# A recurrent mixer's gate products in stacked form, with its zero fills and one weight split at other places

## The reference, cut to what matters

```
proj = x @ w_in
gate_b, gate_c, val_a, val_b, gate_lru = split(proj)      # five times 512 channels
y_a = gate_b * causal_conv3(gate_c * val_a)
xc = causal_conv4(val_b) + conv_b_bias
r = sigmoid(xc_heads @ wa + ba)                           # 8 heads of 64 channels
i = sigmoid(xc_heads @ wx + bx)
log_a = -8 * r * softplus(-lam);  a = exp(log_a)
b = sqrt(-expm1(2 * log_a)) * (i * xc)
h[t] = a[t] * h[t-1] + b[t]
y_b = h * gelu(gate_lru)
m = concat(y_a, y_b) @ w_out
x = layer_norm(ALPHA * x + m)
x = layer_norm(ALPHA * x + hier_moe(x))                   # top-1 group, top-2 experts
```

## Time and profile before

| | |
|---|---|
| median of 3 runs | 1199.74 us (1199.53 to 1200.79) |
| the profiled execution | 1202.03 us, of which its span is 1200.3 |
| mean granted clock of TensorE | 0.977 of full speed |
| TensorE busy | 1121.1 us (93% of the span), 5736 matmuls |
| VectorE busy | 808.0 us (67%) |
| ScalarE busy | 537.6 us (45%) |
| GpSimd busy | 194.2 us (16%) |
| first 497 us | the mixer, 20 rounds |

### The profile page before, as it was taken

One profiled execution on the slowest core, in us unless ns is written; L12 is line 12 of the kernel. 1 busy time (PEld: TensorE's weight loads), 2 busy tenths in 40 slices (PEclk: granted clock), 3 DMA queues, 4 the chain that ended last, 5 costly groups with the idle time before them and its releaser, 6 DMA issues.

```text
span 1200.3 us, 20513 instructions
## 1 busy us (share of the span) xinstructions
PE 1121.1 (93%) x5736; PEld 995.4 (83%) x5737; DVE 808.0 (67%) x1532; ACT 537.6 (45%) x703; POOL 194.2 (16%) x189
## 2 busy tenths in 40 slices
PE   6999999999999999999999988899998999999970
PEld 6999999999999999978888867687887887777760
DVE  4666544374446456767777758797755898888884
ACT  4465343363336346422223312655544666656530
POOL 1000000010001000102222223406101132322322
PEclk9999999999999999999999999899999999999995
DMA  5331599747973742544444225896866789888563
GB/s 182 132 107 50 143 147 121 94 114 115 118 91 122 282 170 85 173 140 156 148 168 141 106 93 190 294 330 220 288 232 236 276 320 354 294 297 292 197 225 140
DMA packets 87274, 221.58 MB, mean 185 GB/s; under 512 B 19152, under 2 KB 45808, under 8 KB 80944
## 3 DMA queue, kind: packets, MB, share of 16 engines
q1 hardware_dynamic: 57824, 129.90, 33.1%
q0 software_dynamic: 18160, 59.53, 14.8%
q10 hardware_dynamic: 11232, 31.47, 13.7%
HBM read 133.75 MB, written 87.11 MB: 184 GB/s over the span
## 4 chain that ended last, share of the span: by engine, by line
PE 53%; DMA 16%; DVE 13%; issue 7%; ACT 6%; ACTq 2%; DVEq 2%; SPq 0%; POOL 0%; POOLq 0%
DMA y_scr<-yb 11%; PE ps_h L1484 9%; PE ps_vb_c L903 8%; PE ps_va_b L292 7%; PE ps_vb_c L292 7%; PE ps_va_b L903 6%; PE ps_o L1462 6%; PE ps_g L292 3%; PE ps_x L1451 2%; DMA gate<-g_scr 2%; DVE w_lo L1117 1%; PE ps_r_i L916 1%; ACT x_hi L1112 1%; PE ps_h L1513 1%; DVE yb L562 1%
## 5 line engine op out<-in xcount | busy, mean ns | idle before, releaser
L1484 PE MATMUL ps_h<-x_hi,xt_hi 128*128 x312 | 125.5, 402 | 3.0 <-issue 2.4
L292 PE MATMUL ps_vb_c<-x_hi,w_hi 128*128 (+1 forms) x320 | 114.6, 358 | 9.7 <-DVE x_lo L467 9.6
L1484 PE MATMUL ps_h<-x_hi,xt_lo 128*128 x312 | 122.0, 391 | 0.0
L1484 PE MATMUL ps_h<-w_lo,xt_hi 128*128 x312 | 121.7, 390 | 0.0
L292 PE MATMUL ps_vb_c<-x_hi,w_lo 128*128 (+1 forms) x320 | 113.9, 356 | 0.0
L292 PE MATMUL ps_vb_c<-x_lo,w_hi 128*128 (+1 forms) x320 | 113.3, 354 | 0.0
L292 PE MATMUL ps_va_b<-x_hi,w_lo 128*128 (+1 forms) x320 | 112.7, 352 | 0.0
L292 PE MATMUL ps_va_b<-x_hi,w_hi 128*128 (+1 forms) x320 | 112.6, 352 | 0.0
L292 PE MATMUL ps_va_b<-x_lo,w_hi 128*128 (+1 forms) x320 | 111.8, 349 | 0.0
L482 DVE SCALAR_TENSOR_TENSOR xc<-vb,par,xc 128x416 f32<-128x416 f32 (+1 forms) x60 | 39.1, 652 | 53.3 <-ACT xc L353 49.5
L1117 DVE TENSOR_TENSOR w_lo<-x_hi_p,x_hi 128x2048 f32 (+1 forms) x30 | 68.5, 2289 | 8.5 <-ACT x_hi L1112 6.8
(11 more groups left out here) (361 smaller groups left out, 2713.4 us busy)
## 6 DMA issues: line engine op xcount, KB each, us to landing
x_hi_p<-in_w SPq DMA_DIRECT2D x48, 1024.0 KB, 7.1
o_scr<-x_raw ACTq DMA_DIRECT2D x42, 512.0 KB, 7.7
w_lo_p<-xs_scr SPq DMA_DIRECT2D x41, 512.0 KB, 5.8
o_scr<-w_lo_p SPq DMA_DIRECT2D x41, 512.0 KB, 6.1
w_raw<-in_w_in POOLq DMA_DIRECT2D x19, 512.0 KB, 3.7
xs_scr<-x_raw ACTq DMA_DIRECT2D x18, 512.0 KB, 10.5
x_raw<-in_x_t SPq DMA_DIRECT2D x20, 416.0 KB, 3.4
x_hi_p<-y_scr SPq DMA_DIRECT2D x16, 512.0 KB, 4.2
```

Source lines behind the costliest of these rows:

```text
L292: mm = pe.matmul(ps[i][:, 0:CHUNK], w[:, i, k], x[:, k, bass.ds(c * CHUNK, CHUNK)], start=(k == 0 and n == 0), stop=(k == KT - 1 and n == 2))
L1484: mm = pe.matmul(ps_h[par][:], x[:, par, k], w[:, bass.ds(at, 1), k].rearrange("p o n -> p (o n)"), start=(k == 0 and n == 0), stop=(k == ...
```

## The change

**Stacked gates.** `xc_hi` and `xc_lo` become one buffer `xc_st` with two columns of operands, one for each head. Operand 0 has the high half of head 0's 64 channels on partitions 0 to 63 and their low half on 64 to 127; operand 1 has head 1's high half on 64 to 127 and its low half on 0 to 63. The weights are laid out to match, the block of a head twice, once under the other, with r in one half of the output's columns and i in the other. So a product sums high and low parts in one go, and two products a head, with `l_hi` and `l_lo`, do what three did: four in place of six a round. The banks become `ps_ri` (head 0: r on the lower partitions, i on the upper) and `ps_ir` (head 1, the other way round). The product of the low halves of both is now in the sum too. ScalarE writes `xc_st` in two operations of 64 partitions, VectorE subtracts in two, and the gate tanh are four operations of 64 partitions. The gate weights of a group come in six small loads on GpSimd.

**Buffers.** The tanh of r goes to `a_t`, not to `yb`; the magnitude lives in the bank `ps_ri` (`mag`), not in `yb`; its Tanh comes ahead of Exp. The wait for the store of `yb` moves from ScalarE's gate tanh to VectorE's scan, which is now the first to write `yb`. TensorE's gates wait for `b_t` of the round before in place of the tanh of i.

**Fills.** They stand in `step` between the tanh of the gelu (and `split(4)`) and the gate tanh, no longer at its start. The frozen ones go to the last chunks of j = 1 and 2, three transfers each.

**Third split.** `split(2)` moves ahead of ScalarE's first tap of `ya`, and on VectorE ahead of the two taps.

```diff
--- before.py
+++ after.py
@@ -112,8 +113,7 @@
...
-    xc_hi = sb("xc_hi", [P, LRU_N], F32R)
-    xc_lo = sb("xc_lo", [P, LRU_N], F32R)
+    xc_st = sb("xc_st", [P, 2, LRU_N], F32R)
...
@@ -133,8 +133,11 @@
...
-    ps_vb, ps_c, ps_va, ps_b, ps_r, ps_i = (t[:, i] for t in (ps_vb_c, ps_va_b, ps_r_i) for i in range(2))
+    ps_vb, ps_c, ps_va, ps_b, ps_ri, ps_ir = (t[:, i] for t in (ps_vb_c, ps_va_b, ps_r_i) for i in range(2))
+
+    low, high = slice(0, HALF), slice(HALF, P)
     ps = [ps_vb, ps_c, ps_va, ps_b, ps_g]
+    mag = ps_ri[:, 0:LRU_N]
...
@@ -196,6 +200,14 @@
...
+    def load_gates(pool, group):
+
+        gate = lambda rows, g, n: w_lru[group, rows, g:g + n, rows].rearrange("o p k n -> p (o k) n")
+        for rows in (low, high):
+            pool.dma_start(w_raw[rows, 1, 0].rearrange("p (k n) -> p k n", n=HALF), gate(low, 0, 2)).then_inc(s_lraw, 16)
+            for g in range(2):
+                pool.dma_start(w_raw[rows, 1, 1:2, (1 - g) * HALF:(2 - g) * HALF], gate(high, g, 1)).then_inc(s_lraw, 16)
...
@@ -203,9 +215,10 @@
...
-            dst = w_raw[:, i % 2] if i < MT else w_raw[:, i % 2, 0:2]
-            src = w_in[i] if i < MT else w_lru[0]
-            pool.dma_start(dst, src).then_inc(s_wraw[i % 2], 16)
+            if i < MT:
+                pool.dma_start(w_raw[:, i % 2], w_in[i]).then_inc(s_wraw[i % 2], 16)
+            else:
+                load_gates(pool, slice(0, 1))
...
@@ -295,10 +307,10 @@
...
             if not start:
-                pe.wait_ge(s_thi, q)
-            for g, bank in enumerate((ps_r, ps_i)):
-                for n, (w, x) in enumerate(((l_hi, xc_hi), (l_hi, xc_lo), (l_lo, xc_hi))):
-                    mm = pe.matmul(bank[:, 0:LRU_N], w[:, g], x[:], start=(n == 0), stop=(n == 2))
+                pe.wait_ge(s_b, q)
+            for head, bank in enumerate((ps_ri, ps_ir)):
+                for n, w in enumerate((l_hi, l_lo)):
+                    mm = pe.matmul(bank[:, 0:LRU_N], w[:, head], xc_st[:, head], start=(n == 0), stop=(n == 1))
...
@@ -318,15 +330,17 @@
...
+            elif i < MT:
+                act.wait_ge(s_wraw[i % 2], 16 * (j * (WP // 2 - i % 2) + (i // 2 + i % 2)))
             else:
-                act.wait_ge(s_wraw[i % 2], 16 * (j * (WP // 2) + (i // 2 + i % 2)))
+                act.wait_ge(s_lraw, 16 * 6 * (j + 1))
...
@@ -358,11 +372,13 @@
...
             act.wait_ge(s_ri, q)
-            act.activation(xc_hi[:], xc[:], ACT.Copy).then_inc(s_xch, 1)
+            act.activation(xc_st[low, 0], xc[low], ACT.Copy)
+            act.activation(xc_st[high, 1], xc[high], ACT.Copy).then_inc(s_xch, 1)
+            if split is not None:
+                split(2)
             act.wait_ge(s_u, q + 1)
             act.activation(ya[:, 0:n], u[:, 0:n], ACT.Copy, scale=col(CA0)).then_inc(s_tapa, 1)
             if split is not None:
-                split(2)
                 split(3)
...
@@ -371,20 +387,24 @@
...
             if split is not None:
                 split(4)
+            if fills is not None:
+                fills()
             act.wait_ge(s_ri, q + 1)
-            act.wait_ge(s_yb_out, 16 * (q + j))
-            act.activation(yb[:], ps_r[:, 0:LRU_N], ACT.Tanh, scale=0.5, bias=hrb[:, bass.ds(j, 1)]).then_inc(s_thr, 1)
+            act.wait_ge(s_h, q)
+            act.activation(a_t[low], ps_ri[low, 0:LRU_N], ACT.Tanh, scale=0.5, bias=hrb[low, bass.ds(j, 1)])
+            act.activation(a_t[high], ps_ir[high, 0:LRU_N], ACT.Tanh, scale=0.5, bias=hrb[high, bass.ds(j, 1)]).then_inc(s_thr, 1)
             act.wait_ge(s_b, q)
-            act.activation(i_t[:], ps_i[:, 0:LRU_N], ACT.Tanh, scale=0.5, bias=hib[:, bass.ds(j, 1)]).then_inc(s_thi, 1)
+            act.activation(i_t[low], ps_ri[high, 0:LRU_N], ACT.Tanh, scale=0.5, bias=hib[high, bass.ds(j, 1)])
+            act.activation(i_t[high], ps_ir[low, 0:LRU_N], ACT.Tanh, scale=0.5, bias=hib[low, bass.ds(j, 1)]).then_inc(s_thi, 1)
             act.wait_ge(s_thr, q + 1)
-            act.wait_ge(s_h, q)
-            act.activation(a_t[:], yb[:], ACT.Exp, scale=nsp4[:, bass.ds(j, 1)], bias=nsp4[:, bass.ds(j, 1)]).then_inc(s_a, 1)
-            act.wait_ge(s_a, q + 1)
-            act.activation(yb[:], yb[:], ACT.Tanh, scale=sp4[:, bass.ds(j, 1)], bias=sp4[:, bass.ds(j, 1)]).then_inc(s_t, 1)
+            act.wait_ge(s_thi, q + 1)
+            act.activation(mag, a_t[:], ACT.Tanh, scale=sp4[:, bass.ds(j, 1)], bias=sp4[:, bass.ds(j, 1)]).then_inc(s_t, 1)
+            act.wait_ge(s_t, q + 1)
+            act.activation(a_t[:], a_t[:], ACT.Exp, scale=nsp4[:, bass.ds(j, 1)], bias=nsp4[:, bass.ds(j, 1)]).then_inc(s_a, 1)
             if split is not None:
                 split(5)
             act.wait_ge(s_z, 2 * q + 2)
-            act.activation(yb[:], yb[:], ACT.Sqrt).then_inc(s_sq, 1)
+            act.activation(mag, mag, ACT.Sqrt).then_inc(s_sq, 1)
...
@@ -422,26 +442,24 @@
...
-        act.wait_ge(s_zero, 1)
-        for i in range(1, 1 + FROZEN):
-            act.dma_start(xs_scr[i * P:(i + 1) * P, :], zero).then_inc(s_zo, 16)
-            act.dma_start(g_scr[i * P:(i + 1) * P, :], zero[:, 0:1]).then_inc(s_zo, 16)
-        for i in range(STORED + (NCH - 2) * OFILL, STEPS - NE):
-            act.dma_start(o_scr[i * P:(i + 1) * P, :], zero).then_inc(s_zo, 16)
+        def fill_frozen(i):
+
+            act.dma_start(xs_scr[bass.ds(i * P, P), :], zero).then_inc(s_zo, 16)
+            act.dma_start(g_scr[bass.ds(i * P, P), :], zero[:, 0:1]).then_inc(s_zo, 16)
+            act.dma_start(o_scr[bass.ds((i + (STORED + (NCH - 2) * OFILL - 1)) * P, P), :], zero).then_inc(s_zo, 16)
+
         with act.Fori(1, GROUPS - 1) as j:
             with act.Fori(0, NCH - 1) as c:
-                fill((j - 1) * (NCH - 1) + c)
-                step(j, c, False, None)
-            step(j, NCH - 1, True, lambda i: split_w(j + 1, i))
-        assert (GROUPS - 2) * (NCH - 1) * 2 == NE and (NCH - 2) * OFILL + STORED <= STEPS - NE and STORED < (-(-(FEWEST - 1) // 2) - FTAIL) * 2 + 2
+                step(j, c, False, None, lambda: fill((j - 1) * (NCH - 1) + c))
+            step(j, NCH - 1, True, lambda i: split_w(j + 1, i), lambda: fill_frozen(j))
...
         with act.Fori(0, NCH - 2) as c:
-            fill_results(c)
-            step(GROUPS - 1, c, False, None)
+            step(GROUPS - 1, c, False, None, lambda: fill_results(c))
...
@@ -484,7 +502,8 @@
...
             dve.wait_ge(s_xch, q + 1)
-            dve.tensor_tensor(xc_lo[:], xc[:], xc_hi[:].bitcast(F32), ALU.subtract).then_inc(s_xcl, 1)
+            dve.tensor_tensor(xc_st[high, 0], xc[low], xc_st[low, 0].bitcast(F32), ALU.subtract)
+            dve.tensor_tensor(xc_st[low, 1], xc[high], xc_st[high, 1].bitcast(F32), ALU.subtract).then_inc(s_xcl, 1)
...
@@ -540,7 +560,7 @@
...
-            dve.scalar_tensor_tensor(out=yb[:], in0=b_t[:], scalar=1.0, in1=yb[:],
+            dve.scalar_tensor_tensor(out=mag, in0=b_t[:], scalar=1.0, in1=mag,
                                      op0=ALU.add, op1=ALU.mult).then_inc(s_z, 1)
...
@@ -559,6 +579,7 @@
...
             dve.wait_ge(s_carry, q + 1)
+            dve.wait_ge(s_yb_out, 16 * (q + j))
             dve.tensor_tensor_scan(yb[:, 0:n], a_t[:, 0:n], b_t[:, 0:n], h_carry[:], ALU.mult, ALU.add).then_inc(s_h, 1)
             dve.wait_ge(s_h, q + 1)
```

19 lines of the change are left out of this document (11 added, 8 removed).

## The result

The changed kernel takes 1230.9 us (median of 4 runs, 1228.21 to 1232.94) where the kernel before takes 1200.3 (median of 4, the three of the table above and one of 1206.2): a ratio of 1.0235, with a 95% interval of 1.0206 to 1.0263. It is 2.35% slower. The forecast was 1203.7, within 1194 to 1211. The profiled execution took 1228.95 us, with a span of 1227.3 and a mean granted clock of 0.969.

The account below looks back on a forecast made before the run. TensorE's own work bound the kernel before; after, the ring of ScalarE and VectorE in the last group. The end's 2.3 plus the clock's 1.7, 4.0 us on the median 1199.74, gave 1203.7 us, range 1194 to 1211.

Parts of the forecast that it names:

- the group's end: At group boundaries: raw weights loaded while fills drain (0 to 4 us each) and six gate loads, both summed as 0.
- TensorE's saving: In the mixer: two gate products fewer in 20 rounds, 7.6 us, of which 7.2 before the last round's own gates.
- The store wait: In j = 1, 2: the wait moved to VectorE's scan costs nothing; all 5.5 us of TensorE's idle time go.
- Rival B: In j = 1, 2 VectorE waits for the store instead, 5.5 us idle stays: 1198 to 1201 us, chance 0.12.
- Rival C: Six GpSimd gate loads at 1.2 us, not 0.54, cost about 4 us at start and two boundaries: 1212 to 1216, chance 0.10.
- Halves: Per round, operations on 64 partitions add 1.5 us on ScalarE (copy 0.5, tanh 1.0) and 0.5 on VectorE.
- my two bounds: An operation on 64 partitions costs between half and the full price of a whole one; the full price was taken.
- the ring: Loop of ScalarE and VectorE from Sqrt to Sqrt in the last group: from 21.56 to 24.9 us, above TensorE's 23.44.
- The start: Round 2 of TensorE begins 2 us later, plus 0 to 3 if the six gate loads are slow.
- The last group: In j = 3 ScalarE and VectorE become the bound; gates late by 0.3, 1.5, 2.7 and 1.1, 5.6 us in sum.
- The end: At the mixer's end the last `yb` is ready at 508.0, 2.3 us later, and TensorE's transposes move equally.
- The clock: After TensorE's idle time of 5 us ahead of the transposes, a lower granted clock loses 1.7 us of full-speed work.

Follow-up runs that it names:

- the run above: The changed kernel with gate weights loaded by one transfer of 128 x 256 in place of six, stacked layout left out: 1215.3 us, ratio 1.0087.
- halves alone: The kernel before, with its copy of `xc`, tanh of r and of i and subtraction each cut into two operations on 64 partitions: 1228.1 us, ratio 1.0189.
- spread fills, stacked gates: The changed kernel with all gate weights loaded early, the 24 result fills spread over rounds, g_scr filled by two transfers: 1199.9 us, ratio 0.9971; again 1200.0, 0.9974.

## Why the prediction was wrong, point by point

The step that failed is the one on the group's end: two costs, the weights loaded while fills drain and the six gate loads, went into the sum at nothing. The other terms follow in the order of the prediction.

**TensorE's saving** (7.2 us): right. Rounds without idle time went from 23.8 to 23.4.

**The store wait** (5.5 us saved, none new): right. No wait on `y_scr<-yb` is left on either engine, and no gate inside j = 1 and 2 is late but the one behind the boundary. Rival B did not come.

**The group's end** (two unknown costs taken as 0, with 4 us kept for the range): this is the step that failed. The two boundaries took 8.2 and 5.7 us more than before, where the forecast had them 0.8 and 1.9 us shorter, by TensorE's saving and the idle time that goes: 16.6 of the 27.2 us by which the time was missed. I had both causes in hand, wrote them down, and took the favourable end for each. The rows even had the measure, 17.39 us for a store behind fills. What I did not see is that a move of 14 us within the round puts that draining just on the last round's loads (8.1 us from issue to landing for the third weight, 9.95 for the last gate load), and that the last of six loads is queued behind fills where one load is ahead of them. Rival C had the right place, and its sign came (the split of `l_hi` waiting over 2 us for DMA), but it had the wrong mechanism: GpSimd issues the six at 0.5 to 0.7 us each, not 1.2. At the boundaries it is their landing that is late, and only beside 4 byte pieces; at the start it is 3.0 us of waiting, where C had 4. That 4 byte pieces hold the queues up stood in no term and in no rival; how they do it stays open.

**Halves** (full price, 0.49 or 0.5 us for each extra one): the size was off, the sign right. Of my two bounds the full price was the nearer one, and the measured price lies beyond it: pairs start 0.57 (copy), 0.62 (tanh) and 0.60 (subtraction) apart, so four tanh and their successor take 2.57 where two took 0.99. The gates to the Sqrt came to 5.36 us, not 4.9, and the ring to 26.17, not 24.9. My bounds went by half and full, and left out that a pair might lose its overlap. Whole operations, with g_scr in one piece, took 0.0093 off the ratio and all idle time out of the last group.

**The start** (+2 us, 0 to 3 more): it became 4.8 (+4.0, and the saving of two rounds). Round 2 starts at 63.6, as forecast (63.9), but what follows it runs at the lower clock at first (0.68 and 0.89 in the two stretches of 4 us from 63.3 on, 1.7 us of work), which I had not counted. With one load it was 48.5 in the run above, but with halves alone, and one load too, 53.0: both can bring it, and their shares stay open.

**The last group** (idle 0.3, 1.5, 2.7, 1.1 us): the mechanism was right, the ring of ScalarE and VectorE is the bound and whole operations set TensorE free. The sizes were 0.8, 2.2, 3.3 and 0.1, with 7.4 ahead of them from the boundary.

**The end** (+2.3 us): +24.5, since all of the above comes before it. The way from the last gates to the transposes was to grow from 23.2 to about 30.6 by the forecast's own figures (490.7 to 521.3); it took 29.8.

**The clock** (1.7 us): right in size, 1.4 us, for a reason that isn't shown, since after a pause of 2.87 us in another run the clock was lower still. And it was counted once only. The idle times of 3.2 us and more at the start, at the boundaries and in the last group each brought a stretch with products 0.35 apart in place of 0.19 (granted clock 0.68, 0.50, 0.51 and 0.57 over some 4 us), the 2.2 us at 461 did not (1.00); the round behind the first boundary took 25.3 us for it, not 23.4, with no idle time in it.

## What to carry to other kernels

Before an operation is cut into pieces on fewer partitions, count each piece at its full price, and the overlap with its neighbour as lost, and look at who stands behind it: here four such cuts cost 0.9 to 1.9%, and the products that they saved were 0.6% of TensorE's time. Where a queue of transfers is moved within a round, lay its whole drain time, not its issue time, over every load that is needed just in time. And when two unknown costs meet at one place, price them together from the worst row that is there, rather than taking zero for each.

## What the runs showed of the hardware

- A tanh of 420 columns takes 0.60 us on ScalarE on 64 partitions as on 128, and neighbours of 64 partitions start 0.61 to 0.64 us apart where those of 128 start 0.49 to 0.51 apart. On VectorE the halves follow after 0.60.
- Two transfers of 512 bytes in 128 pieces of 4 bytes, among four of 512 KB, left the transfer engines at 0 to 67 GB/s for 6.5 and 7.2 us; as one piece each, the same fills ran at 400 GB/s. That was worth 1.8% of the changed kernel, and nothing measurable in the kernel before, where it took away ScalarE's 38.8 us of waiting for stores and brought the transposes 2.8 us forward.
- The length of TensorE's pause ahead of the transposes does not settle at which of its two levels (1.2 and 2.4 GHz) it comes back. Over the next 4 us the granted clock was 0.58 after 4.06 us (spread fills, stacked gates) and 0.66 after 4.25 (the changed kernel), and 1.00 after 2.75 (the kernel before) and 3.08 (only its fills moved). But it was 0.57 after 2.87, in the kernel before with g_scr in one piece, and 0.67 after 2.45, in the changed kernel with the same:

```profile
516.20:520.20 4.00, 4.00 (x15) 3.48 (x16) 1.71 (x4) 1.02 (x1) 0.00 (x0) 0.57 0.50 181
```

```profile
523.20:527.20 4.00, 4.00 (x17) 3.31 (x18) 1.72 (x4) 1.02 (x1) 0.00 (x0) 0.67 0.52 192
```
